# S5 matrices of a hybrid encoder layer kept as 64x64 blocks without zeros, on one Trainium2 core

## The chip, the core and the metric

The kernel runs as one program on one core of a Trainium2 chip. The metric is the device time of one execution in microseconds (us). Before the change the median of three runs is 1902.22 us (1891.05 to 1905.71).

## What is computed

Two layers of an encoder trunk over 528 positions of 1024 channels (16 meta tokens and 512 frames). Each layer projects a normed input into gates and three mixers (gated linear attention, an S5 state space model, sliding window attention), gates and projects each, merges them and adds the result to the residual. The change is in the S5 mixer:

```python
bu_re = einsum('blgi,gni->blgn', ug, bb_re); bu_im = einsum('blgi,gni->blgn', ug, bb_im)
_, _, x_re, x_im = associative_scan(complex_affine_combine, (ab_re, ab_im, bu_re, bu_im), axis=1)
y = einsum('blgn,gin->blgi', x_re, c_re) - einsum('blgn,gin->blgi', x_im, c_im)
y = gelu(y.reshape(B, L, 1024) + d_skip * u)
return y * sigmoid(y @ w_glu)
```

There are 64 groups g of 16 channels i, each with its own complex state of 64 entries n. A group's input matrix is 16 channels to 64 states, its output matrix 64 states to 16 channels. Nothing passes from one group to another.

## The kernel before, in words

**Blocks.** Nearly all of the work is in projections of 1024 by 128 weights, which the program calls blocks. A block's weights come by a DMA that SP issues (`load_block`), ScalarE rounds them (`hi_part`), GpSimd makes the rest (`lo_part`), and TensorE runs 48 matmuls of 264 columns (`project`, L825; L784 and L806 where it follows its input). Three weight buffers are in turn. The list `BLOCKS` sets the order for all engines; each engine runs its own program in that order and waits on semaphores.

**S5 in steps of four.** The scan runs over 132 steps of 4 positions. With the 4 positions folded in, a pair of groups has 2 x 16 channels x 4 = 128 inputs, 2 x 64 = 128 states, and 128 outputs. So each pair (`q` of `QUADS` = 4, eight `j` per layer) has three 128x128 matrices: `mbt` (inputs to states, re and im), `cam` (states to outputs, re and im) and `toep` (inputs of the same step to outputs). Since two groups share one matrix and don't mix, half of each is zero.

**The matrices are built on the core**, for layer 0 in the first blocks (m = 0, during the `gk`, `gv` and `gq` blocks) and for layer 1 at the end of layer 0 (m = 1, after `sg` 2, `ws5` 0, 1, 2, 3, 5 and `wout` 0, 2, 4; `MATS_0`, `MATS_1`). For each j: VectorE (`s5_matrices`) makes products and adds them, per half of the partitions, into `cam` and `mbm`, whose zeros GpSimd has written once, and signals `mats_ready`; TensorE (`step_matrices`, run by `mat_turn` after its block) transposes `mbm` (L881), multiplies `cam` by it (L888, four strips of 32 columns) and turns the next C (L871); ScalarE (`matrices_out`, in its own `mat_turn`) moves both to SBUF and SP spills them to DRAM (`spill_mats`, six DMAs). A buffer is used again when its spill has landed (`spilled`).

**They are used** during the `ag`, `mg2` and `watt` blocks (`S5F`): ScalarE's queue loads the matrices of one j (`load_mats`), TensorE makes the state inputs (`step_inputs`, two `aux` results of 8 matmuls in all, L1164), VectorE scans (`s5_scan`), TensorE makes the outputs (`step_outputs`, 12 matmuls, L1177 and L1179), ScalarE applies the GELU into `Z4` (L1538). In one turn `step_outputs(j)` and `step_inputs(j+1)` follow each other, with two blocks between turns. `AX_` (`aux`) is PSUM in two halves that are taken in turn (`aux_take` waits until the result before last in that half was read).

## Time and profile before

| | |
|---|---|
| median of 3 runs | 1902.22 us |
| the profiled execution | 1898.04 us, of which its span is 1896.2 us |
| TensorE matmuls (PE) | 1762.7 us busy, 93% of the span |
| weight loads (PEld) | 1572.6 us, beside the matmuls |
| VectorE (DVE) | 961.6 us, 51% |
| ScalarE (ACT) | 693.6 us, 37% |
| GpSimd (POOL) | 794.6 us, 42% |
| DMA | 230.38 MB, mean 121 GB/s |

The chain of waits goes through TensorE for 66% of the span, VectorE 10%, DMA 7%, GpSimd 6%. TensorE is the bound in most of the span; the places where it stands idle are the ones to look at, and in the stretches where S5 matrices are built or used most of these are found. Each f32 matmul leaves two records of LDWEIGHTS and two of MATMUL in the trace, so that 12 matmuls are 24 records; a transpose leaves one.

### The profile page before, as it was taken

How to read it: one execution, taken by the hardware profiler on the slowest of the kernel's cores; microseconds unless marked ns; L12 is line 12 of the kernel's file. 1: busy time of each engine (PE TensorE's matmuls, PEld its weight loads, DVE VectorE, ACT ScalarE, POOL GpSimd, SP SyncE). 2: the span in 40 equal slices, each digit the busy share in tenths (PEclk: the TensorE clock that was granted, in tenths of full speed). 3: DMA queues.
4: the chain of work that ended last, by engine and by line, in shares of the span. 5: the costliest groups of instructions: out<-in, count | busy, mean ns of one | idle time of the engine just before them, and what ended most of it. 6: DMA issues, size and time to landing. Idle time of an engine off the chain costs nothing.

```text
span 1896.2 us, 28935 instructions
## 1 busy us (share of the span) xinstructions
PE 1762.7 (93%) x11959; PEld 1572.6 (83%) x11959; DVE 961.6 (51%) x1527; ACT 693.6 (37%) x1236; POOL 794.6 (42%) x492
## 2 busy tenths in 40 slices
PE   6977898999998999999997999989999799999997
PEld 5876798999887999999996987777788688888886
DVE  8997124423428985277653222533243688734223
ACT  3453332444543213233333543344456222224222
POOL 2644565433224324433343686653332332344442
PEclk8898899999999999999998999999999999999999
DMA  9455236222364573436552433542223656433432
GB/s 148 135 167 149 82 88 142 74 79 69 89 152 148 190 200 99 104 90 174 172 156 61 125 90 90 118 123 70 76 79 102 180 191 184 141 100 91 144 104 85
DMA packets 360137, 230.38 MB, mean 121 GB/s; under 512 B 49604, under 2 KB 346744, under 8 KB 357448
## 3 DMA queue, kind: packets, MB, share of 16 engines
q1 hardware_dynamic: 349480, 198.40, 39.8%
q10 hardware_dynamic: 10528, 30.15, 4.7%
q8 instruction: 95, 1.56, 0.4%
q14 instruction: 34, 0.28, 0.1%
HBM read 180.82 MB, written 47.15 MB: 120 GB/s over the span
## 4 chain that ended last, share of the span: by engine, by line
PE 66%; DVE 10%; DMA 7%; POOL 6%; ACT 4%; SPq 3%; issue 3%; ACTq 0%; DVEq 0%; POOLq 0%
PE ring L825 49%; DMA sb_w_raw<-in_w_in 5%; POOL sb_w_lo L667 3%; PE ring L784 3%; DVE sb_s_prod L1572 2%; DVE sb_s_mat_prod L1572 2%; PE aux L1177 2%; PE ring L806 1%; PE aux L1085 1%; SPq L570 1%; PE aux L1164 1%; PE aux L1130 1%; DVE sb_s_rot L2071 1%; PE aux L1106 1%; DVE sb_o_branch L1655 1%
## 5 line engine op out<-in xcount | busy, mean ns | idle before, releaser
L667 POOL TENSOR_TENSOR sb_w_lo<-sb_w_raw,sb_w_hi 128x1024 fp32r<-128x1024 f32 x246 | 608.7, 2476 | 1018.3 <-ACT sb_w_hi L1229 1016.2
L1229 ACT ACTIVATE sb_w_hi<-sb_w_raw 128x1024 fp32r<-128x1024 f32 x246 | 259.9, 1057 | 623.5 <-DMA sb_w_raw<-in_w_in 394.4
L825 PE MATMUL ring<-sb_u_hi,sb_w_hi 128*128 128x264 f32 (+1 forms) x2112 | 362.9, 325 | 31.5 <-DVE sb_tmp_dve L1642 21.4
L825 PEld LDWEIGHTS ring<-sb_u_hi,sb_w_hi 128*128 128x128 f32 x2112 | 308.6, 199 | 70.1 <-DVE sb_tmp_dve L1642 23.8
L825 PE MATMUL ring<-sb_u_lo,sb_w_hi 128*128 128x264 f32 (+1 forms) x2112 | 338.2, 311 | 0.0
L825 PE MATMUL ring<-sb_u_hi,sb_w_lo 128*128 128x264 f32 (+1 forms) x2112 | 334.5, 309 | 0.0
L825 PEld LDWEIGHTS ring<-sb_u_lo,sb_w_hi 128*128 128x128 f32 x2112 | 298.8, 191 | 21.2
L825 PEld LDWEIGHTS ring<-sb_u_hi,sb_w_lo 128*128 128x128 f32 x2112 | 294.2, 188 | 20.9
L1261 ACT ACTIVATE sb_tmp_act<-ring 128x528 f32<-128x528 f32 (+1 forms) x112 | 67.4, 602 | 133.0 <-PE ring L825 130.1
L825 PE MATMUL ring<-sb_y_hi,sb_w_hi 128*128 128x264 f32 (+1 forms) x504 | 88.1, 325 | 3.1 <-ACT sb_w_hi L1229 3.1
L1492 ACT ACTIVATE sb_att_scores<-sb_att_scores,sb_att_neg_max 128x208 f32<-128x208 f32 x128 | 58.4, 458 | 82.1 <-DVE sb_att_neg_max L1860 82.1
L825 PE MATMUL ring<-sb_y_lo,sb_w_hi 128*128 128x264 f32 (+1 forms) x504 | 87.4, 324 | 0.0
L825 PE MATMUL ring<-sb_y_hi,sb_w_lo 128*128 128x264 f32 (+1 forms) x504 | 86.3, 321 | 0.0
L825 PEld LDWEIGHTS ring<-sb_y_hi,sb_w_hi 128*128 128x128 f32 x504 | 73.5, 190 | 10.2 <-issue 3.2
L825 PEld LDWEIGHTS ring<-sb_y_lo,sb_w_hi 128*128 128x128 f32 x504 | 74.7, 192 | 7.3
L825 PEld LDWEIGHTS ring<-sb_y_hi,sb_w_lo 128*128 128x128 f32 x504 | 73.6, 188 | 7.3
L1572 DVE TENSOR_TENSOR sb_y_lo<-sb_o_branch,sb_y_hi 128x528 fp32r<-128x528 f32 (+1 forms) x48 | 50.3, 1065 | 50.7 <-ACT sb_y_hi L1245 50.2
L1677 DVE SCALAR_TENSOR_TENSOR sb_tmp_dve<-sb_tmp_act,ring 128x528 f32<-128x528 f32 (+1 forms) x32 | 22.3, 696 | 98.3 <-PE ring L825 86.1
L1642 DVE SCALAR_TENSOR_TENSOR sb_tmp_dve<-sb_tmp_act,ring 128x528 f32<-128x528 f32 (+1 forms) x32 | 22.2, 694 | 86.0 <-ACT sb_tmp_act L1261 85.5
L1245 ACT ACTIVATE sb_y_hi<-sb_o_branch 128x528 fp32r<-128x528 f32 (+1 forms) x48 | 29.6, 634 | 77.4 <-DVE sb_o_branch L1649 48.7
L1664 DVE SCALAR_TENSOR_TENSOR sb_s_out<-sb_tmp_act,sb_s_out 128x528 f32<-128x528 f32 (+1 forms) x16 | 25.0, 1562 | 63.9 <-ACT sb_tmp_act L1261 63.9
L1677 DVE SCALAR_TENSOR_TENSOR sb_mix<-sb_tmp_act,ring 128x528 f32<-128x528 f32 (+1 forms) x16 | 11.1, 696 | 84.4 <-PE ring L825 76.2
(328 smaller groups left out, 2585.4 us busy)
## 6 DMA issues: line engine op xcount, KB each, us to landing
sb_w_raw<-in_w_in SPq DMA_DIRECT2D x166, 512.0 KB, 4.1
sb_s_loaded<-s_matrices ACTq DMA_DIRECT2D x16, 1808.0 KB, 8.1
s_matrices<-sb_s_phase SPq DMA_DIRECT2D x16, 528.0 KB, 3.2
s_matrices<-sb_s_mbt SPq DMA_DIRECT2D x16, 512.0 KB
s_matrices<-sb_s_ca SPq DMA_DIRECT2D x16, 512.0 KB
sb_w_raw<-in_w_gla_out SPq DMA_DIRECT2D x16, 512.0 KB, 3.8
sb_w_raw<-in_w_attn_out SPq DMA_DIRECT2D x16, 512.0 KB, 3.8
sb_w_raw<-in_s_w_glu SPq DMA_DIRECT2D x16, 512.0 KB, 3.7
```

The lines of the kernel that those rows point to most:

```text
L667: pool.tensor_tensor(WL[:, w], WR[:, w], WH[:, w].bitcast(F32), ALU.subtract).then_inc(lo_ready, 1)
L784: last = pe.matmul(RING[:, 2 * r + hf, 0:c1 - c0], w[:, n % SLOTS, kt, :], moving(b[0], xx[:, kt], c0, c1), start=(term == 0 and kt == 0), ...
L825: last = pe.matmul(RING[:, 2 * r + hf, 0:c1 - c0], w[:, n % SLOTS, kt, :], moving(b[0], xx[:, kt], c0, c1), start=(term == 0 and kt == 0), ...
L1177: pe.matmul(dst, cam[:, ri, q], XX[:, ri, q, :], start=(ri == 0), stop=False)
L1229: act.activation(WH[:, w], WR[:, w], ACT.Copy).then_inc(hi_ready, 1)
L1245: act.activation(YH[:, j, t0:], src[:, t0:], ACT.Copy).then_inc(yhi_ready, 1)
L1261: act.activation(two(TA[:, t % 2], t0), ps, ACT.Tanh, scale=0.5).then_inc(done, 1)
L1492: act.activation(SC[:, u % 2, hd], SC[:, u % 2, hd], ACT.Exp, bias=NMX[:, hd:hd + 1], accum_out=SMM[:, hd:hd + 1])
L1572: return dve.tensor_tensor(o, a, b, op)
L1642: dve.scalar_tensor_tensor(two(td, t0), two(TA[:, t % 2], t0), 1.0, ps, ALU.add, ALU.mult).then_inc(free, 1)
L1664: dve.scalar_tensor_tensor(zj, TA[:, t % 2, t0:].rearrange("p (s c) -> p s c", s=STRIDE), 1.0, zj, ALU.add, ALU.mult).then_inc(glu_used, 1)
L1677: dve.scalar_tensor_tensor(two(td, t0), two(TA[:, t % 2], t0), 1.0, ps, ALU.add, ALU.mult).then_inc(free, 1)
```

## The change

The zeros are left out. The rows of the stationary and moving tiles are ordered by group (64 rows of one group, then 64 of the other) instead of by position, so a pair's matrices become two dense 64x64 blocks each. `mbt`, `cam` and `toep` are half as large (`S5_FLOATS` 3616 before, 2336 now). In pairs with odd `q` the two groups' state halves are exchanged, so that a matmul of an odd pair reads rows of one half and writes the other half. What each engine does instead:

- TensorE: each 128x128 matmul of `step_inputs` and `step_outputs` becomes two of 64x64 with the same 132 columns (16 and 24 in all). `step_outputs` starts with `toep` instead of `cam`, and has three waits on its own semaphore `row_tiles_done`. The eight transposes of `mbm` become 16 matmuls of 64x64 by 64 columns; the eight 32-column matmuls have 64 columns instead of 128 and wait for `first_power`.
- ScalarE: before the old work of a turn, four copies build `mb0`, a small zero-padded copy of `mbm`, and signal `first_power`; the C copies are four instead of two. `load_mats` issues three DMAs instead of one.
- VectorE: two full-height operations in place of four of half height, twice per j; at the start of the program four more copies before `dt_wide`, and six in place of two after it.
- SP, DMAs: `load_b` 8 instead of 2 per layer, `Z4` loads 8 instead of 4, `YD` stores 2 per j instead of 1, `YZ` loads 8 per part instead of 4.
- GpSimd: `cam` and `mbm` need no zeros, `toep` and `mb0` do.

The core of the diff:

```diff
-S5_FLOATS = 2 * QUADS * P + 2 * QUADS * P + QUADS * P + 2 * QUADS * STEPS
+S5_FLOATS = 2 * QUADS * 64 + 2 * QUADS * 64 + 2 * QUADS * STEPS + QUADS * 64
...
+        def load_b(queue, m):
+
+            for ri, src in enumerate((s5_b_re, s5_b_im)):
+                dst = MB[m]["b"][:, ri].rearrange("p (a x) i -> p a x i", x=2)
+                src = src[m].rearrange("(a x g) n i -> x g n a i", x=2, g=2)
+                for g in range(2):
+                    for x in range(2):
+                        rows = slice(S5_STATE * (g ^ x), S5_STATE * (g ^ x) + S5_STATE)
+                        queue.dma_start(dst[rows, :, x], src[x, g]).then_inc(s5_par, 16)
...
                 for ri in range(2):
                     for q in range(QUADS):
-                        last = pe.transpose(AX_[:, 2 * h + ri, P * q:P * q + P],
-                                            MB[m]["mbm"][:, ri, q].rearrange("p a b -> p (a b)"), ID[:])
+                        for g in range(2):
+                            ins, outs = half_rows(g ^ (q % 2)), half_rows(g)
+                            c0 = 128 * ri + 64 * (q // 2)
+                            last = pe.matmul(AX_[outs, 2 * h + q % 2, c0:c0 + 64],
+                                             MB[m]["mbm"][ins, ri, q].rearrange("p a b -> p (a b)"), ID[ins, ins],
+                                             start=True, stop=True)
                 last.then_inc(aux_full[h], 1)
                 h = aux_take(m, ("toep", j))
-                cam, mbm = MB[m]["cam"][:, j % 2], MB[m]["mbm"]
+                cam, mb0 = MB[m]["cam"][:, j % 2], MB[m]["mb0"]
+                pe.wait_ge(first_power, 8 * m + j + 1)
...
+                        for a in range(2):
+                            for x in range(2):
+                                for g in range(2):
+                                    ins, outs = half_rows(g), half_rows(g ^ x)
+                                    last = pe.matmul(AX_[outs, 2 * h + x, STEPS * a:STEPS * a + STEPS],
+                                                     mbt[ins, ri, 2 * a + x, :], Z4[ins, j, 2 * a + x, :],
+                                                     start=True, stop=True)
                         last.then_inc(aux_full[h], 1)
 
                 def step_outputs(j):
 
-                    pe.wait_ge(x_state, 8 * ly + j + 1)
...
+                    for a in range(2):
+                        n = 3 * (8 * ly + j) + 2 * a + 1
+                        if a:
+                            last.then_inc(row_tiles_done, 1)
+                            pe.wait_ge(row_tiles_done, n - 1)
+                        for x in range(2):
+                            for g in range(2):
+                                rows, q = half_rows(g), 2 * a + x
+                                last = pe.matmul(AX_[rows, 2 * h + x, STEPS * a:STEPS * a + STEPS],
+                                                 toep[rows, q], Z4[rows, j, q, :], start=True, stop=False)
+                        last.then_inc(row_tiles_done, 1)
+                        pe.wait_ge(row_tiles_done, n)
+                        pe.wait_ge(x_state, 8 * ly + j + 1)
                         for ri in range(2):
-                            pe.matmul(dst, cam[:, ri, q],
-                                      XX[:, ri, q, :], start=(ri == 0), stop=False)
-                        last = pe.matmul(dst, toep[:, q], Z4[:, j, q, :],
-                                         start=False, stop=True)
+                            for x in range(2):
+                                for g in range(2):
+                                    ins, q = half_rows(g ^ x), 2 * a + x
+                                    last = pe.matmul(AX_[half_rows(g), 2 * h + x, STEPS * a:STEPS * a + STEPS],
+                                                     cam[ins, ri, q], XX[ins, ri, q, :],
+                                                     start=False, stop=(ri == 1))
...
             def matrices_out(m, j):
 
+                act.wait_ge(mats_ready, 8 * m + j + 1)
+                for half in range(2):
+                    rows = slice(64 * half, 64 * half + 64)
+                    for x in range(2):
+                        c0 = S5_GROUP * (half ^ x)
+                        last = act.activation(MB[m]["mb0"][rows, :, x::2, c0:c0 + S5_GROUP],
+                                              MB[m]["mbm"][rows, :, x::2, 0], ACT.Copy)
+                last.then_inc(first_power, 1)
                 if j:
                     spilled(act, m, j - 1)
...
-                act.dma_start(MSB[:, j % 2], MATD[ly, j]).then_inc(mats_in[j % 2], 16)
+                o = S5_FLOATS - QUADS * 64
+                act.dma_start(MSB[:, j % 2, 0:o], MATD[ly, j, :, 0:o]).then_inc(mats_in[j % 2], 16)
+                toep = mat_part(MATD[ly, j], "toep").rearrange("(t g i) x -> g t i x", t=STRIDE, g=2)
+                for g in range(2):
+                    act.dma_start(MSB[64 * g:64 * g + 64, j % 2, o:], toep[g]).then_inc(mats_in[j % 2], 16)
...
-                    for g in range(2):
-                        rows = slice(64 * g, 64 * g + 64)
-                        cols = slice(S5_GROUP * g, S5_GROUP * g + S5_GROUP)
-                        tt(o_re[rows, :, :, cols], t[0][rows], t[1][rows], ALU.subtract)
-                        if negate:
-                            last = dve.scalar_tensor_tensor(
-                                o_im[rows, :, :, cols].rearrange("p q n i -> p (q n) i"),
-                                t[2][rows].rearrange("p q n i -> p (q n) i"), -1.0,
-                                t[3][rows].rearrange("p q n i -> p (q n) i"), ALU.mult, ALU.subtract)
-                        else:
-                            last = tt(o_im[rows, :, :, cols], t[2][rows], t[3][rows], ALU.add)
+                    flat = "p q n i -> p (q n) i"
+                    tt(o_re, t[0], t[1], ALU.subtract)
+                    if negate:
+                        last = dve.scalar_tensor_tensor(o_im.rearrange(flat), t[2].rearrange(flat), -1.0,
+                                                        t[3].rearrange(flat), ALU.mult, ALU.subtract)
+                    else:
+                        last = tt(o_im, t[2], t[3], ALU.add)
                     link(last)
```

TensorE in the second build, from the end of block `ws5` 0 (L784) through its turn to the next block (L825), before (`sb_s_mb` is `mbm`, `sb_s_ca` is `cam`, in brackets the semaphores waited for):

```order
L881 MATMUL aux<-sb_identity,sb_s_mb_134 128x128 [waits aux_free0,mats_ready]
L881 MATMUL aux<-sb_identity,sb_s_mb_134 128x128 x7
L888 MATMUL aux<-sb_s_ca_137,sb_s_mb_134 32x128 [waits aux_free1]
L888 MATMUL aux<-sb_s_ca_137,sb_s_mb_134 32x128 x7
L891 MATMUL aux<-sb_s_skip_diag_144,sb_identity 128x32
L871 MATMUL aux<-sb_identity,sb_s_c_in_143 128x128 [waits c_loaded0]
L871 MATMUL aux<-sb_identity,sb_s_c_in_143 128x128
L825 MATMUL ring<-sb_u_hi,sb_w_hi 128x264 [waits hi_ready,slot_free1]
```

and of the change, at the same place:

```order
L902 MATMUL aux<-sb_identity,sb_s_mb_137 64x64 [waits aux_free0,mats_ready]
L902 MATMUL aux<-sb_identity,sb_s_mb_137 64x64 x15
L911 MATMUL aux<-sb_s_ca_140,sb_s_mb_first_148 32x64 [waits first_power,aux_free1]
L911 MATMUL aux<-sb_s_ca_140,sb_s_mb_first_148 32x64 x7
L914 MATMUL aux<-sb_s_skip_diag_147,sb_identity 128x16
L889 MATMUL aux<-sb_identity,sb_s_c_in_146 128x128 [waits c_loaded0]
L889 MATMUL aux<-sb_identity,sb_s_c_in_146 128x128
L840 MATMUL ring<-sb_u_hi,sb_w_hi 128x264 [waits hi_ready,slot_free1]
```

Between its two groups of matmuls TensorE now waits for ScalarE's `first_power`; the next block stands behind that wait.

ScalarE in the same turn, where its rows now read (`sb_s_mb_first` is `mb0`, `sb_mix_hi` the rounding of the merged sum after block `ws5` 0):

```order
L1271 ACTIVATE sb_w_hi<-sb_w_raw 128x1024 [waits w_loaded0]
L1492 ACTIVATE sb_mix_hi<-sb_mix 128x528 [waits mix_ready]
L1341 ACTIVATE sb_s_mb_first_148<-sb_s_mb_137 64x4x16 [waits mats_ready]
L1341 ACTIVATE sb_s_mb_first_148<-sb_s_mb_137 64x4x16 x3
L1347 ACTIVATE sb_s_mbt_139<-aux 128x2x4x64 [waits aux_full0]
L1351 ACTIVATE sb_s_toep_143<-aux 128x64 [waits aux_full1]
L1365 ACTIVATE sb_s_c_0_144<-aux 64x64 [waits aux_full1,mats_ready]
L1365 ACTIVATE sb_s_c_0_144<-aux 64x64 x3
```

The two rows of L1341 are new; ahead of them stand, as before, a weight block's rounding and a wait for `mix_ready`, which VectorE gives after TensorE has ended block `ws5` 0.

TensorE in the turns of the scan stage (`step_outputs(0)`, then the first half of `step_inputs(1)`), of the change:

```order
L1211 MATMUL aux<-sb_s_steps,sb_s_loaded 64x132 [waits aux_free0]
L1211 MATMUL aux<-sb_s_steps,sb_s_loaded 64x132 x3
L1220 MATMUL aux<-sb_s_state,sb_s_loaded 64x132 [waits x_state,row_tiles_done]
L1220 MATMUL aux<-sb_s_state,sb_s_loaded 64x132 x7
L1211 MATMUL aux<-sb_s_steps,sb_s_loaded 64x132 [waits row_tiles_done]
L1211 MATMUL aux<-sb_s_steps,sb_s_loaded 64x132 x3
L1220 MATMUL aux<-sb_s_state,sb_s_loaded 64x132 [waits x_state,row_tiles_done]
L1220 MATMUL aux<-sb_s_state,sb_s_loaded 64x132 x7
L1193 MATMUL aux<-sb_s_steps,sb_s_loaded 64x132 [waits aux_free1,mats_in1]
L1193 MATMUL aux<-sb_s_steps,sb_s_loaded 64x132 x7
```

Before, these were 12 matmuls of 128x132 behind one wait for `x_state`, then 4; now 24 behind four waits, three of them for TensorE's own matmuls, then 8.

## Rows read from the trace of the kernel before

**Rows 1.** Windows: us; busy us per engine (instructions); TensorE clock, DMA share, GB/s
```profile
84.00:182.00 98.00, 70.06 (x565) 63.75 (x564) 88.96 (x145) 42.62 (x67) 49.69 (x54) 0.85 0.51 143
...
836.00:1010.00 174.00, 167.00 (x1420) 163.00 (x1420) 109.26 (x169) 56.74 (x85) 65.64 (x29) 0.97 0.53 150
```

**Rows 2.** Timeline of TensorE, one turn of the scan stage: start, duration, records
```profile
639.51 0.61 PE L1177 MATMUL aux<-sb_s_state,sb_s_loaded 128*128 128x132 f32 x4
...
642.21 2.03 PE L1164 MATMUL aux<-sb_s_steps,sb_s_loaded 128*128 128x132 f32 x16
643.99 2.18 PE L825 MATMUL ring<-sb_y_hi,sb_w_hi 128*128 128x264 f32 x16
```

**Rows 3.** Lines L888, L1117: ns min/median/max of a record; timeline of narrow matmuls
```profile
L888 PE MATMUL aux<-sb_s_ca,sb_s_mb x256: 272/273/423, 91.2 to 989.9; 128*32 128x128 f32 x128
...
857.67 0.64 PE L888 MATMUL aux<-sb_s_ca,sb_s_mb 128*32 128x128 f32 x16
...
L1117 PE MATMUL aux<-sb_att_pt_a,sb_att_v_a x8: 216/218/264, 384.7 to 384.9; 16*64 16x64 f32 x8
...
384.67 0.45 PE L1117 MATMUL aux<-sb_att_pt_a,sb_att_v_a 16*64 16x64 f32 x8
...
242.24 2.00 PE L992 MATMUL aux<-sb_gla_v_tok,sb_gla_k_tok 64*128 64x256 f32 x16
```

**Rows 4.** Timeline of the scan stage: GELU after an output, second input half waiting
```profile
609.60 0.61 ACT L1538 ACTIVATE sb_s_steps<-aux 128x528 f32<-128x528 f32 x1 [0.26 <-PE aux L1179]
...
626.81 1.17 PE L1164 MATMUL aux<-sb_s_steps,sb_s_loaded 128*128 128x132 f32 x8 [0.18 <-ACT sb_s_steps L1538]
```

**Rows 5.** First build: VectorE's timeline; TensorE's waits in all; chain of waits
```profile
103.92 1.70 DVE L1572 TENSOR_TENSOR sb_s_mat_prod<-sb_s_c,sb_s_powers 128x320 f32<-128x320 f32 x4 [1.95 <-DMA s_matrices<-sb_s_toep]
105.65 0.48 DVE L1572 TENSOR_TENSOR sb_s_ca<-sb_s_mat_prod 64x320 f32<-64x320 f32 x1
...
176.42 1.52 DVE L1572 TENSOR_TENSOR sb_s_mb<-sb_s_mat_prod 64x256 f32<-64x256 f32 x4
...
PE aux L881 <- DVEq L2041: 29.8, 9, 5.8
...
112.48 4.28 DMA s_matrices<-sb_s_toep
```

**Rows 6.** First build: timeline of ScalarE and TensorE after block gv 2
```profile
102.08 1.09 PE L881 MATMUL aux<-sb_identity,sb_s_mb 128*128 128x128 f32 x8 [2.22 <-DVEq L2041]
...
106.81 1.01 ACT L1297 ACTIVATE sb_s_mbt<-aux 128x1024 f32<-128x1024 f32 x1
```

**Rows 7.** Second build: timeline of TensorE
```profile
836.12 3.89 PE L825 MATMUL ring<-sb_u_hi,sb_w_hi 128*128 128x264 f32 x16 [2.93 <-DVE sb_tmp_dve L1642]
...
870.38 1.04 PE L881 MATMUL aux<-sb_identity,sb_s_mb 128*128 128x128 f32 x8
...
922.88 2.73 PE L825 MATMUL ring<-sb_y_hi,sb_w_hi 128*128 128x264 f32 x16 [3.06 <-ACT sb_w_hi L1229]
```

**Rows 8.** Second build: timeline of ScalarE
```profile
859.40 1.01 ACT L1297 ACTIVATE sb_s_mbt<-aux 128x1024 f32<-128x1024 f32 x1
...
873.71 1.01 ACT L1297 ACTIVATE sb_s_mbt<-aux 128x1024 f32<-128x1024 f32 x1
...
874.77 0.55 ACT L1313 ACTIVATE sb_s_c<-aux 64x128 f32<-64x128 f32 x2
...
906.77 1.06 ACT L1229 ACTIVATE sb_w_hi<-sb_w_raw 128x1024 fp32r<-128x1024 f32 x1 [12.67 <-DMA sb_w_raw<-in_w_s_out]
```

**Rows 9.** Start of the scan stage: chain of waits; DMA issues with KB and us to landing
```profile
557.66 13.40 DMA sb_w_raw<-in_w_in
...
sb_s_loaded<-s_matrices ACTq DMA_DIRECT2D x16, 1808.0 KB, 8.1
```

**Rows 10.** Start of the program: timeline of VectorE
```profile
17.53 0.29 DVE L1608 COPY sb_s_params<-aux 128x128 f32<-128x128 f32 x1 [0.93 <-PE aux L944]
...
28.33 0.71 DVE L1615 TENSOR_SCALAR sb_tmp_dve<-aux 128x528 f32<-128x528 f32 x1 [0.25 <-PE aux L847]
```

147 lines of the change are left out of this document (82 added, 65 removed).

## The prediction, made before the changed kernel was run

> **What bounds the kernel now.** I read the page's engine shares first: TensorE is busy for 93% of the span, so a saving on another engine counts only where TensorE waits for it, and TensorE's own records count nearly in full. Then the windows. In the first build (84 to 182 us) TensorE is busy for 70.06 of 98 us at a granted clock of 0.85, VectorE for 88.96: VectorE bounds it. In the second (836 to 1010) TensorE is busy for 167.0 of 174, VectorE for 109.26: TensorE bounds it [rows 1]. In the scan stage the timeline has one turn: outputs from 639.51 to 642.21, inputs to 643.99, then a block without a gap [rows 2]. Last the waits: TensorE waits 29.8 us in nine places for VectorE's `mats_ready` [rows 5]. So three parts of the change can move the end: records on TensorE in the scan stage, VectorE's work in the first build, and in the second whatever puts a wait into a stretch that has nearly none.
>
> The sum is made on the profiled execution (1898.04 us), 4.2 us below the median of the runs.
>
> **Scan stage, records (16 turns).** Outputs take 2.70 us for 24 records and inputs 1.78 for 16 [rows 2]: 0.112 each, together 4.48 a turn. The change has 48 and 32 records, each a 64x64 tile of the same 132 columns. If they didn't overlap at all a turn would take 9 us. The nearest rows say that they do: matmuls of 32 weight columns (four column strips) start (0.64-0.27)/15 = 0.025 us apart with 128 moving columns, those of 64 weight columns (0.45-0.218)/7 = 0.033 [rows 3]. Full overlap of four tiles would be 0.112/4 = 0.028, of two 0.056. I take 0.033 for inputs and `cam` products (32 records each, 1.06 each) and 0.056 for `toep`, which uses only two of the four quadrants (16 records, 0.90): 3.02. To this come three waits of TensorE for itself. Each costs the time from a matmul's start to its end (0.27 by the shortest record of its size [rows 3]) and a restart, which I take as 0.1, in all 0.38: 1.14. I add 0.3 for changes between tile shapes and rounding, which no row shows. 4.46 against 4.48: the turn doesn't get shorter. Bounds: 80 records at 0.028 and no extra make 3.4 (-17 us over 16 turns), all at 0.056 make 5.9 (+23).
>
> The row with 64 weight rows and 256 columns, 16 records in 2.00 us (0.125 each) [rows 3], is at 0.0625 per 128 columns; there two row halves overlap, but they write to two banks of PSUM. In the change both row halves write to one bank in every group of four tiles. No row has that. By the Trainium skill ("TensorEngine Tiling (Array Packing)", Restrictions and Gotchas), different row tiles cannot access one PSUM bank at the same time; by that rule the turn would be the 5.9 and not the 4.46.
>
> **Scan stage, the GELU.** TensorE waits 0.18 us for the GELU of the outputs before it makes the second half of inputs (8 matmuls after the first 8) [rows 4]. The first half lasted 8 x 0.112 = 0.9 and will last 0.5; the outputs end the same. A GELU takes 0.61 and starts 0.26 after TensorE [rows 4]. So the wait grows by what the first half shrinks, 0.4, in 14 to 16 turns: +6. It is lost in full, since the next block stands behind it. Range 0 to +7.
>
> **Loads.** The matrices of one j shrink from 1808 KB, landed in 8.1 us [rows 9], to 2336/3616 of it, 1168 KB. At the start of the scan stage the chain goes for 13.40 us through a weight transfer which lands beside the first matrices [rows 9]. A third of the matrix bytes less: -2 per layer, -4 (0 to -6). Three issues in place of one on ScalarE lie under blocks of TensorE.
>
> **First build (8 matrices).** VectorE writes `ca` and `mb` in half-height operations of 0.48; two full ones replace four, twice: the 0.48 saved twice in each, 1.0 for `ca` and 0.8 for `mb` [rows 5], 1.8 a matrix. At most 14 us. Three things take it back. TensorE's second group of matmuls now needs `first_power`, four copies on ScalarE. After `gv` 2 ScalarE is at 106.81 us with that turn's work, behind the decay's functions, while TensorE was ready at 102.08 [rows 6]; I count a stall of 5 in each of three such turns, partly in place of a wait for the next matrix (5.8 the longest [rows 5]). The next matrix starts not when VectorE is free but when `toep` has been spilled and landed, 4.28 us in the chain, and VectorE waits 1.95 for it [rows 5]: less VectorE time makes that wait longer. And VectorE has ten copies of 0.29 in place of two at the start of the program, with 0.25 us to spare [rows 10]: 8 x 0.29 = 2.3, less that and less some cover by loads, +1.6. Saved are 8 x 1.8 = 14.4; three stalls of 5 come to +15, of which I take off what they replace, waits for the next matrix that shrink by about 4 each, -12; the longer wait for `toep` takes back 8; with the 1.6 the stage ends about 1.5 us earlier (-14.4+15-12+8+1.6 = -1.8). Range -8 to +4. The transposes are 16 records in place of 8, at half the columns: nothing.
>
> **Second build (8 matrices).** Here `first_power` decides. After `sg` 2 and five `ws5` blocks and before the next block TensorE does its turn. After `ws5` 0 the transposes start at 870.38, and ScalarE, which first rounds the merged sum (`mix_ready`), comes to its part at 873.71, 3.3 later [rows 7, 8]. Until now nobody waited for it. Now the four copies come first: about 0.25 each by the C copies of 64x128 (0.55 for two [rows 8]), 1.0 in all, so that TensorE's second group may start 4.3 after the first, of which it fills 1.2: a stall of 3.1. After `sg` 2 (ScalarE's part at 859.40 [rows 8], second group of TensorE at 857.67 [rows 3]) it is 1.7+1.0 = 2.7 less a start that moves with the copies, 2.4. After `ws5` 2, ScalarE stands before a weight block that lands late and is rounded at 906.77 (idle 12.67 [rows 8]); the turn's transposes begin near 900, so the stall is 906.77+1.06+1.0-901 = 8. For the other turns I take, by the nearest of these, 3.1 after `ws5` 1, 2.4 after one more, and 1 after each of two `wout`, where ScalarE is free and its copies run beside the transposes: 2.4+3.1+3.1+8+2.4+1+1 = 21, one turn at nothing. Taken off: waits of TensorE for VectorE and ScalarE in this stage which the new stall covers. They are 2.93 and 3.06 with slowed blocks behind them (3.89 and 2.73 for the 16 records that take 2.18 elsewhere [rows 2, 7]), and 1.9 of `mats_ready`: -8. Idle stretches of 2.9 and more are followed by blocks at the low clock, which I charge the new ones of 3.1 and 8 with 2. The sum is 21-8+2 = 15; I take +14, since a delay of one turn leaves ScalarE more time before the next. Range +2 (ScalarE is waited for only for the 1.0 of its copies, and the 8 taken off) to +25 (nothing taken off).
>
> **Costed at nothing:** `load_b`, `Z4`, `YD` and `YZ` issues, hidden by blocks (SP stands in no wait of TensorE in the rows); GpSimd's zeros, in its idle time; 32 narrow records in a build turn, the same columns in all.
>
> **Sum.** 0 + 6 - 4 - 1.5 + 14 = +14: 1898 + 14 = **1912 us**.
>
> **Rivals.**
> 1. *Forecast*: stalls for `first_power` outweigh VectorE's saving, and the scan stage gives nothing. 1912, own range 1898 to 1924. Chance 0.50.
> 2. *The quadrants overlap in full and ScalarE is in time.* For it: 0.025 is in a row already. Scan turn 2.2+1.1 = 3.3 instead of 4.46, -18, GELU +8, loads -5, first build -5, second +5: 1883 (1872 to 1893). Against: ScalarE's late starts are in the rows. Chance 0.18. This one ends faster.
> 3. *Two row halves do not write to one bank together.* Every record of the scan stage costs 0.056: 80 x 0.023 less the `toep` already so priced, 64 x 0.023 = 1.5 a turn, +23 on the forecast, less 3 of the GELU's 6, as the first half of the inputs covers it again: 1932. Its place is `step_inputs` and the `cam` products. It decides from 0.045 a record on, where +12 is reached. For it the skill's rule above; against it nothing, as all rows have separate banks. Chance 0.20. It ends slower.
> 4. *The wait feeds back.* In the second build ScalarE's rounding of the next weights stands behind its copies, TensorE behind both, and six of the turns lose 3 and as much as a slowed block (1.7, from 3.89 against 2.18 [rows 2, 7]), with one more of 8, less the 8 taken off: +28 in place of +14: 1926. It decides from a ScalarE that comes 2.9 late in four turns or more. Chance 0.12.
> 5. *It doesn't do what it says*: weights of 64 rows load no faster, so a record costs 0.112 and nothing overlaps. 9 us a turn: +72, 1980. The rows of L888 and L992 speak against it; left out of the range.
>
> **How the numbers follow.** Range 1884 to 1936: half of case 2 lies below or at its end, cases 3 and 4 mostly inside, case 5 outside. A difference of 1% (19 us) is what a measurement can tell from no change, so faster is below 1883 and slower above 1921. Faster: half of case 2, 0.10. Slower: case 3 with 0.18, case 4 with 0.08, an eighth of case 1, 0.06, in all 0.32. The rest, 0.58, is within.
>
> **What would show it.** In the trace after: (a) TensorE waiting for ScalarE's copy L1341 at L911 in the second build, about 20 us in all over eight places, and the window from `sg` 2 to `wout` 4 some 14 us longer; (b) records of L1193 and L1220 0.033 apart and the turn about 4.5 us; 0.056 is case 3, 0.028 case 2; (c) a wait for the GELU of about 0.6 before the second half of L1193; (d) VectorE's busy time lower by 1.8 per matrix (29 us over both builds), while the first build ends within a few us of 182. I am wrong if ScalarE's copies run before TensorE's transposes end in most turns, or if the first build shrinks by 8 us or more, which would mean that the spill of `toep` wasn't what held VectorE.

## The result, and the profile after

The changed kernel takes 1921.5 us (median of 4 runs, 1920.58 to 1929.08) where the kernel before, run beside it, takes 1900.86. The ratio is 1.0107, with a 95% interval of 1.0081 to 1.0132: slower by 1.1%. One run of the experiment e3 below (2004.83 us) was slower at a lower clock and is left out of its row. The forecast was 1912 us, +14 on the profiled execution; the measured time is inside the range, 9 us above its middle. The profiled execution has a span of 1918.8 us against 1896.2, +22.6.

The page's engine shares show less work, not more, on TensorE and VectorE:

```profile
span 1918.8 us, 31149 instructions
...
PE 1748.8 (91%) x12985; PEld 1539.8 (80%) x12985; DVE 930.4 (48%) x1471; ACT 701.7 (37%) x1332; POOL 787.4 (41%) x490
```

TensorE is busy for 14 us less than before and the span is 22.6 longer, so TensorE stands idle for some 36 us more. The waits of TensorE (engine, line, whom for: us in total, times, longest) say where:

```profile
PE aux L911 <- ACT sb_s_mb_first L1341: 32.3, 12, 6.3
PE ring L840 <- DVE sb_tmp_dve L1707: 19.9, 8, 6.1
PE aux L1193 <- DMA sb_s_steps<-s_in_rows: 17.3, 2, 9.3
...
PE aux L902 <- DVEq L2102: 12.3, 4, 5.6
```

Two entries are new: `first_power`, 32.3 us, which the forecast had, and the loads of `Z4`, 17.3 us, which it had costed at nothing (before, TensorE waited 0.4 for them in layer 0, and 1.4 at the same place in layer 1). The wait for `mats_ready` fell from 29.8 [rows 5] to 12.3.

Following the same event through both timelines gives the account. Each number is how much later (+) the event comes than before:

| event | before, us | later by | this stretch |
|---|---|---|---|
| first block | 35.64 | +2.7 | +2.7 |
| last `mbm` transposes of the first build | 178.32 | -3.3 | -6.0 |
| TensorE ready for the first `step_inputs` | 569.2 | -9.0 | -5.7 |
| first `step_inputs` (569.64 before) | 569.64 | -1.4 | +7.6 |
| last `step_outputs` of layer 0 | 724.98 | -0.6 | +0.8 |
| first `mbm` transposes of the second build | 856.71 | -1.0 | -0.4 |
| last of them | 988.59 | +13.2 | +14.1 |
| block before layer 1's `step_inputs` | 1482.63 | +14.7 | +1.5 |
| its first `step_inputs` | 1486.02 | +22.7 | +8.0 |
| end | 1896.2 | +22.6 | -0.1 |

The second build cost 14.1, and two waits for `Z4` cost 15.5. All else together is -7, and not all of that is the change's: in e3 below, whose program is that of before up to the `Z4` loads, TensorE is ready at 565.98 and so 3.2 us earlier than before. The windows that answer to [rows 1], with the columns given there:

```profile
84.00:182.00 98.00, 70.33 (x810) 66.93 (x809) 77.81 (x117) 50.24 (x115) 55.22 (x58) 0.84 0.41 108
...
836.00:1010.00 174.00, 156.69 (x1526) 153.79 (x1527) 88.78 (x136) 55.84 (x122) 58.33 (x24) 0.93 0.41 115
```

In the first build VectorE has 11 us less to do (88.96 before), TensorE gets no further for it. In the second, TensorE's busy share is down from 167.0 to 156.7, and its clock from 0.97 to 0.93. The timeline there, the turn after block `ws5` 0, answers to [rows 7, 8]; first TensorE:

```profile
873.19 0.69 PE L902 MATMUL aux<-sb_identity,sb_s_mb 64*64 64x64 f32 x32
876.54 0.43 PE L911 MATMUL aux<-sb_s_ca,sb_s_mb_first 128*32 128x64 f32 x16 [2.65 <-ACT sb_s_mb_first L1341]
...
877.31 3.72 PE L840 MATMUL ring<-sb_u_hi,sb_w_hi 128*128 128x264 f32 x16
```

and ScalarE:

```profile
875.05 0.64 ACT L1492 ACTIVATE sb_mix_hi<-sb_mix 128x528 fp32r<-128x528 f32 x1 [3.04 <-DVE sb_mix L1627]
875.60 0.79 ACT L1341 ACTIVATE sb_s_mb_first<-sb_s_mb 64x64 f32<-64x64 f32 x4
```

ScalarE waits for the merged sum until 875.05, rounds it, then makes `mb0`. TensorE stood since 873.9. The 16 records behind the wait take 3.72 us and not 2.18 [rows 2]: they ran mostly at the low level of the clock (1.2 GHz), as the granted clock of 0.54 in that stretch shows (third last number, here and in the other windows):

```profile
877.30:881.00 3.70, 3.70 (x20) 3.70 (x19) 3.63 (x8) 1.82 (x6) 1.39 (x1) 0.54 0.44 121
```

So a wait of 2.65 costs 4.2 here. The turn after `ws5` 2, where ScalarE stands before a late weight block, is the longest:

```profile
915.06 0.65 PE L911 MATMUL aux<-sb_s_ca,sb_s_mb_first 128*32 128x64 f32 x16 [6.30 <-ACT sb_s_mb_first L1341]
```

The scan stage's turn of [rows 2], in the changed kernel:

```profile
640.79 0.67 PE L1211 MATMUL aux<-sb_s_steps,sb_s_loaded 64*64 64x132 f32 x8
641.53 0.68 PE L1220 MATMUL aux<-sb_s_state,sb_s_loaded 64*64 64x132 f32 x16
642.30 0.67 PE L1211 MATMUL aux<-sb_s_steps,sb_s_loaded 64*64 64x132 f32 x8
643.03 0.68 PE L1220 MATMUL aux<-sb_s_state,sb_s_loaded 64*64 64x132 f32 x16
643.53 0.63 PE L1193 MATMUL aux<-sb_s_steps,sb_s_loaded 64*64 64x132 f32 x16
644.44 0.68 PE L1193 MATMUL aux<-sb_s_steps,sb_s_loaded 64*64 64x132 f32 x16 [0.28 <-ACT sb_s_steps L1593]
645.05 2.22 PE L840 MATMUL ring<-sb_y_hi,sb_w_hi 128*128 128x264 f32 x16
```

A record takes 0.273 us from start to end (median of L1220). So 16 records in 0.68 or 0.63 start (0.68-0.27)/15 = 0.027 apart, or 0.024: four tiles at once. The eight `toep` records are (0.67-0.27)/7 = 0.057 apart: two. From the last start of one group to the first of the next are 641.53-(640.79+7x0.057) = 0.34 us, which is the price of one of TensorE's own waits. From the last start of the first half of the inputs (643.53+0.63-0.27 = 643.89) to the first start of the second half are 0.55 us: the wait for the GELU, 0.28 behind the end of the last matmul, costs about 0.5 in starts. The whole turn is 645.05-640.79 = 4.26 us against 4.48.

The first `step_inputs`, after TensorE stood for the loads, and SP's queue (start, length, issues) as it issues them:

```profile
568.25 2.04 PE L1193 MATMUL aux<-sb_s_steps,sb_s_loaded 64*64 64x132 f32 x32 [7.99 <-DMA sb_s_steps<-s_in_rows]
```

```profile
540.88 9.22 SPq L621 DMA_DIRECT2D sb_s_steps<-s_in_rows  x8
```

SP's eight issues take 9.2 us where four took 4.7, but not 1.15 us each (ns min/median/max, before and after):

```profile
L610 SPq DMA_DIRECT2D sb_s_steps<-s_in_rows x8: 318/646/2604, 549.9 to 1468.0; - x8
...
L621 SPq DMA_DIRECT2D sb_s_steps<-s_in_rows x16: 319/487/2877, 540.9 to 1488.7; - x16
```

The first five take 0.32 to 0.49 us, and only the last three 1.9 to 2.4, while the earlier loads are under way. What is long is the loads: in layer 0 from the first issue to the last landing 27.3 us (540.88 to 568.19), where before they took 19.7 (549.89 to 569.60), and in layer 1 28.0 against 13.7. A window of 8 us while the loads run, of before (issues from 549.89) and of after:

```profile
551.00:559.00 8.00, 8.00 (x67) 7.62 (x64) 0.59 (x1) 1.94 (x3) 2.39 (x1) 1.00 1.18 190
```

```profile
551.00:559.00 8.00, 8.00 (x68) 8.00 (x67) 0.00 (x0) 0.00 (x0) 0.00 (x0) 1.00 1.26 115
```

The last column is GB/s: 190 with loads of 32 partitions, 115 with loads of 16, and the DMA engines are taken up in both (1.18 and 1.26).

### The profile page after: what moved, and what is told of

It is laid out like the page before. It is cut to its first block, busy times and chain, and to the rows that moved or that the text cites. A ratio compares the mean times of both kernels' runs of the same rounds, so it can differ in the third digit from the quotient of the medians.

```text
span 1918.8 us, 31149 instructions
## 1 busy us (share of the span) xinstructions
PE 1748.8 (91%) x12985; PEld 1539.8 (80%) x12985; DVE 930.4 (48%) x1471; ACT 701.7 (37%) x1332; POOL 787.4 (41%) x490
## 4 chain that ended last, share of the span: by engine, by line
PE 65%; DVE 12%; POOL 6%; DMA 6%; ACT 5%; issue 3%; SPq 3%; ACTq 0%; DVEq 0%; POOLq 0%
PE ring L840 50%; DMA sb_w_raw<-in_w_in 4%; POOL sb_w_lo L682 3%; PE ring L799 3%; DVE sb_s_prod L1627 3%; PE ring L821 2%; PE aux L1111 1%; DVE sb_s_rot L2132 1%; SPq L579 1%; DVE sb_s_rot L1627 1%; PE aux L1220 1%; SPq L621 1%; DVE sb_s_state L1627 1%; PE aux L1132 1%; PE aux L1156 1%
## 5 line engine op out<-in xcount | busy, mean ns | idle before, releaser
L840 PE MATMUL ring<-sb_u_hi,sb_w_hi 128*128 128x264 f32 (+1 forms) x2112 | 372.1, 331 | 29.6 <-DVE sb_tmp_dve L1707 19.9
L840 PEld LDWEIGHTS ring<-sb_u_hi,sb_w_hi 128*128 128x128 f32 x2112 | 317.1, 204 | 69.3 <-DVE sb_tmp_dve L1707 22.4
L1729 DVE SCALAR_TENSOR_TENSOR sb_s_out<-sb_tmp_act,sb_s_out 128x528 f32<-128x528 f32 (+1 forms) x16 | 21.7, 1355 | 67.7 <-ACT sb_tmp_act L1303 67.7
L1627 DVE TENSOR_TENSOR sb_s_mat_prod<-sb_s_bbar,sb_s_powers 128x256 f32<-128x256 f32 x64 | 48.5, 818 | 11.0 <-PE aux L889 10.5
```

Of the source, the lines that this page charges most:

```text
L840: last = pe.matmul(RING[:, 2 * r + hf, 0:c1 - c0], w[:, n % SLOTS, kt, :], moving(b[0], xx[:, kt], c0, c1), start=(term == 0 and kt == 0), ...
L1627: return dve.tensor_tensor(o, a, b, op)
L1729: dve.scalar_tensor_tensor(zj, TA[:, t % 2, t0:].rearrange("p (s c) -> p s c", s=STRIDE), 1.0, zj, ALU.add, ALU.mult).then_inc(glu_used, 1)
```

## The experiments

Times and ratios of all, each against runs of the kernel before on the same chip:

| kernel | median us | before beside it | ratio (95%) |
|---|---|---|---|
| changed | 1921.50 | 1900.86 | 1.0107 (1.0081 to 1.0132) |
| e1 `mb0` by VectorE | 1899.35 | 1904.33 | 0.9979 (0.9961 to 0.9996) |
| e2 `Z4` on two queues | 1916.37 | 1904.33 | 1.0058 (1.0026 to 1.0091) |
| e3 before, `Z4` in eight | 1916.26 | 1904.33 | 1.0074 (1.0040 to 1.0109) |
| e4 `Z4` in rows | 1898.32 | 1904.33 | 0.9963 (0.9942 to 0.9983) |
| e5 e1 and e4 | 1875.81 | 1904.32 | 0.9855 (0.9821 to 0.9889) |
| e6 before, `Z4` in rows | 1905.73 | 1904.32 | 1.0010 (0.9988 to 1.0032) |
| e7 e5, half heights | 1893.14 | 1904.32 | 0.9935 (0.9912 to 0.9957) |
| e8 rows, 16 partitions | 1930.20 | 1904.32 | 1.0144 (1.0110 to 1.0178) |
| e9 e1, copies kept | 1902.92 | 1902.63 | 0.9990 (0.9973 to 1.0008) |
| e10 e5, early copies | 1872.81 | 1902.63 | 0.9840 (0.9813 to 0.9866) |
| e11 e5 again | 1876.56 | 1902.63 | 0.9855 (0.9831 to 0.9879) |

A hundredth of the ratio is 19 us.

**e1: no wait for `first_power`.**

```diff
                 h = aux_take(m, ("toep", j))
-                pe.wait_ge(first_power, 8 * m + j + 1)
...
                 products(BB[:, :, qs], 4, MBM[:, 0], MBM[:, 1], False)
+                for half in range(2):
+                    rows = slice(64 * half, 64 * half + 64)
+                    for x in range(2):
+                        c0 = S5_GROUP * (half ^ x)
+                        dve.tensor_copy(MB[m]["mb0"][rows, :, x::2, c0:c0 + S5_GROUP], MBM[rows, :, x::2, 0])
```

and ScalarE's four copies with their wait are gone.

> The changed kernel, but VectorE writes mb0 (four 64x64-element copies behind its other work of a matrix, before mats_ready), and TensorE's wait for first_power is gone. Theory: the 16.9 us that TensorE waits for ScalarE's copies in the second build (five waits, 2.6 to 6.3 us) are the whole loss of that stage, so it gets about 14 us shorter again; in the first build the 15 us of such waits partly turn back into waits for VectorE, which has 8 x 4 short copies more (3 to 5 us): 0 to -4. In all about 1905 us, ratio to the kernel before 1.001 to 1.004. Rival: TensorE would have stood there anyway (for mats_ready, for weights that come late): then the waits move to other lines and the time stays within 5 us of the changed kernel, ratio above 1.008.

1.0107 became 0.9979, about -24 us: more than I expected, and far from the rival. The turn of above is now

```profile
865.16 0.69 PE L902 MATMUL aux<-sb_identity,sb_s_mb 64*64 64x64 f32 x32
865.79 0.43 PE L910 MATMUL aux<-sb_s_ca,sb_s_mb_first 128*32 128x64 f32 x16
...
866.56 2.20 PE L840 MATMUL ring<-sb_u_hi,sb_w_hi 128*128 128x264 f32 x16
```

without a gap and at full clock. From the first to the last transposes the second build takes 124.3 us (851.99 to 976.31), against 146.0 in the changed kernel and 131.9 before. So `first_power` cost 21.7 there, and what the stage saves otherwise, hidden behind it, is 7.6. About half of the 7.6 is in the turns themselves: from the transposes to the next block are 1.40 us (865.16 to 866.56) where before they were 1.96 (870.38 to 872.34), 0.56 in each of seven turns. Waits for `mats_ready` of 1.9 us in all are gone too. In the first build the same stretch went from 86.8 to 78.9 us, 89.0 before; I had expected at most 4 us there.

**e9: ScalarE's copies kept, the wait taken away.** As e1, but ScalarE still makes four copies per matrix, of a constant into a buffer that nobody reads.

```diff
-                        last = act.activation(MB[m]["mb0"][rows, :, x::2, c0:c0 + S5_GROUP],
-                                              MB[m]["mbm"][rows, :, x::2, 0], ACT.Copy)
+                        last = act.activation(MB[m]["spare"][rows, :, x::2, c0:c0 + S5_GROUP],
+                                              ID[rows, 0:64].rearrange("p (r a i) -> p r a i", r=2, a=2), ACT.Copy)
```

> As the kernel in which VectorE writes mb0, but ScalarE still does its four copies per matrix (of a constant, into a buffer nobody reads), and TensorE doesn't wait for them. Theory: it is the wait that costs, with the low clock behind it, not the 0.8 us of ScalarE's time per matrix: like e1, ratio to the kernel before 0.996 to 1.000. Rival: the copies make ScalarE's weight roundings late, and that is what stopped TensorE: then at least half of the 22 us comes back, ratio above 1.003.

0.9990, with an interval that overlaps that of e1: at most a few of the 24 us are ScalarE's own time. It is the wait that costs.

**e3: the kernel before with the `Z4` loads alone in eight.**

```diff
-                            sp.dma_start(Z4[32 * p:32 * p + 32].rearrange("i j q c -> i (j q) c"),
-                                         ZD[ly, :, :, STRIDE - 1 - p, :].rearrange("j (q i) c -> i (j q) c", q=QUADS)
-                                         ).then_inc(steps_loaded, 16)
+                            for g in range(2):
+                                r0 = 32 * p + 16 * g
+                                sp.dma_start(Z4[r0:r0 + 16].rearrange("i j q c -> i (j q) c"),
+                                             ZD[ly, :, :, STRIDE - 1 - p, :]
+                                             .rearrange("j (q g i) c -> g i (j q) c", q=QUADS, g=2)[g]
+                                             ).then_inc(steps_loaded, 16)
```

> The kernel before, with one edit: each of its four Z4 loads of 32 partitions is issued as two of 16 partitions. Theory: this edit alone costs what the changed kernel loses there, 8 us per layer where the wait was 0.4 and 0: +8 to +16 us, ratio 1.004 to 1.009. Rival: the wait comes from the matrix loads in pieces of 256 bytes, or from TensorE's having been early (by 9 us in layer 0) only: then the time is that of the kernel before within 3 us.

+0.7%, 14 us, from an edit that moves the same bytes to the same places. TensorE's waits for these loads:

```profile
PE aux L1167 <- DMA sb_s_steps<-s_in_rows: 18.8, 2, 9.6
```

**e2: the eight loads on two queues.** The four of the second half are issued by ScalarE, beside SP's.

```diff
-                        for g in range(2):
+                        for g in range(1):
                             for p in range(STRIDE):
...
+                        for p in range(STRIDE):
+                            r0 = 64 + 16 * p
+                            act.dma_start(Z4[r0:r0 + 16].rearrange("i j q c -> i (j q) c"),
+                                          ZD[ly, :, :, STRIDE - 1 - p, :]
+                                          .rearrange("j (q g i) c -> g i (j q) c", q=QUADS, g=2)[1]
+                                          ).then_inc(steps_loaded, 16)
```

> The changed kernel, but of the eight Z4 loads the four of the second row half are issued from ScalarE's queue, at the same time as SP issues the other four. Theory: the waits of 8.0 and 9.3 us for Z4 at the start of the scan stage come from transfers of 16 partitions, one after the other on one queue, at 100 to 125 GB/s in place of 180; two queues have 32 partitions under way, and the waits fall to below 1 us, less what later work takes: -12 to -17 us, ratio 0.999 to 1.004. Rival 1: only SP's issue time (9.2 us in place of 4.7) matters: then the same, but the rate during the loads stays at 100 to 125 GB/s and the wait keeps 3 to 4 us each. Rival 2: the DMA engines bound it, whatever the queue: under 4 us in all, ratio above 1.008.

TensorE waits as long as in the changed kernel:

```profile
PE aux L1193 <- issue: 16.6, 2, 8.9
```

But it no longer waits for `Z4`. SP's four issues take 1.91 us, and the last `Z4` load lands at 564.40 (ScalarE's, issued at 546.56), 5.5 us before TensorE's first matmul at 569.87; in layer 1 it is 1502.65 and 1507.06. From the first issue to the last landing the loads take 21.6 and 23.2 us in place of 27.3 and 28.0. What is left for TensorE to wait for is `mats_in`: the first matrices, which ScalarE now issues behind its four `Z4` loads, from 550.69 on, and whose last packet ends at 569.01. (In the changed kernel their last packet ends at 567.29, 0.9 us before the last `Z4` load lands, so that little more than that was to be had here.) So the run doesn't settle how far two queues help. While both move `Z4` the rate is

```profile
550.00:554.00 4.00, 4.00 (x35) 4.00 (x34) 1.41 (x2) 0.61 (x1) 1.09 (x1) 1.00 1.24 141
```

141 GB/s: more than the 108 to 115 of the one queue, and far from 190. None of the three expectations came as stated: the waits are as long as the second rival has them, but for another reason than the `Z4` loads, and the ratio of 1.0058 lies below its 1.008. The ratio is 0.5% lower than the changed kernel's, with intervals that overlap, and I can't say whether anything of that is real. For two transfers to separate halves the Trainium skill ("DMA: Bandwidth & Descriptors", Rules for kernel authors) says that they share the same engines, so "Use one 128-partition transfer"; e4 does so, with 10.9 us from the first issue to the last landing against 21.6 here.

**e4: the same data in four loads of 128 partitions.** The inputs are spilled in the order of `Z4`'s rows, so that a load can take all rows.

```diff
-                            sp.dma_start(ZD[ly, j], Z[:, j]).then_inc(z_spilled, 16)
+                            for t in range(STRIDE):
+                                sp.dma_start(ZD[ly, QUADS * j:QUADS * j + QUADS, :, STRIDE - 1 - t]
+                                             .rearrange("q g i c -> (q g) i c"), Z[:, j, t]).then_inc(z_spilled, 16)
...
+                        for j in range(0, KT, 2):
+                            sp.dma_start(Z4[:, j:j + 2].rearrange("r j q c -> r (j q) c"),
+                                         ZD[ly, QUADS * j:QUADS * j + 2 * QUADS]
+                                         .rearrange("b g t i c -> (g t i) b c")
+                                         ).then_inc(steps_loaded, 16)
```

> The changed kernel, but the spilled S5 inputs lie in DRAM in the order of Z4's rows, so that Z4 comes in four loads of 128 partitions (two j each) in place of eight of 16; the stores before it are 32 of 66 KB in place of 8 of 264 KB. Theory: the loads run at 180 GB/s or more and cost SP under 5 us, so both waits (8.0 and 9.3) go: -13 to -18 us, ratio 0.998 to 1.003. Rival: the four stores of the last j land later and the load is bound by its 528-byte pieces whatever its partitions: under 5 us, ratio above 1.008.

-27 us on the changed kernel by the ratios. TensorE's wait for these loads is gone. The loads were issued from 546.23 on and landed by 557.08, and the window in which they run reads

```profile
548.00:554.00 6.00, 6.00 (x52) 6.00 (x51) 1.28 (x2) 0.61 (x1) 1.73 (x1) 1.00 1.18 310
```

310 GB/s. The gain is more than the 15.5 us of waits. The weights of the next blocks stand behind these loads on SP's queue and in the DMA engines. It fits this that from the first `step_inputs` to the first `step_outputs` are 34.6 and 33.4 us in the two layers, where the changed kernel has 38.7 and 37.2; but it wasn't tried apart.

**e8: partitions or place in DRAM?** The new order in DRAM, but eight loads of 16 partitions; the diff is against e4.

```diff
-                        for j in range(0, KT, 2):
-                            sp.dma_start(Z4[:, j:j + 2].rearrange("r j q c -> r (j q) c"),
+                        for g in range(2):
+                            for t in range(STRIDE):
+                                r0 = 64 * g + 16 * t
+                                sp.dma_start(Z4[r0:r0 + 16].rearrange("i j q c -> i (j q) c"),
+                                             ZD[ly, :, g, t].rearrange("b i c -> i b c")
```

> The changed kernel with the new spill order in DRAM, but still eight loads of 16 partitions each (each row piece 528 bytes as in all versions; 16 rows are now neighbours in DRAM). Theory: the number of partitions of a load sets its rate, not where its pieces lie in DRAM: both waits stay (7 to 10 us each), total within 5 us of the changed kernel, ratio 1.007 to 1.012. Rival: neighbouring pieces in DRAM were what made the four loads fast: the waits fall below 2 us, ratio 0.995 to 1.001.

```profile
547.00:553.00 6.00, 6.00 (x52) 6.00 (x51) 1.41 (x2) 0.61 (x1) 1.36 (x1) 1.00 1.25 111
```

The place in DRAM isn't what made e4's loads fast: in loads of 16 partitions the rate is back at 111 GB/s, the waits are 23.6 us, and the ratio is 1.0144. That is a little above the 1.012 I had as the upper end, as the waits of 11.5 and 12.0 us are above my 10. (The loads are also half as large as e4's; size and partitions weren't varied apart.)

**e5 and e11: both mends.** Their diffs are those of e1 and e4.

> The changed kernel with both edits that helped: VectorE writes mb0 (no wait for first_power), and Z4 is loaded in four loads of 128 partitions from inputs spilled in row order. Theory: the two losses lie in different stages, so their mends add up: -22 and -23 us on the changed kernel, about 1877 us where the kernel before takes 1901, ratio 0.985 to 0.989. Rival: both made TensorE earlier at the same later wait (the weights of the scan stage, VectorE's scan), and only one of them counts in full: ratio above 0.992.

> The kernel with both mends once more, beside e10 on the same chip: 0.983 to 0.989 of the kernel before, as the first time.

0.9855 twice. The two add up (-0.0128 and -0.0144 give 0.9835, which lies inside both intervals), and this version beats the kernel before by 1.5%, 27 us.

**e6: the new spill order in the kernel before.** So that the gain isn't put down to the wrong edit.

```diff
+                            for t in range(STRIDE):
+                                sp.dma_start(ZD[ly, QUADS * j:QUADS * j + QUADS, STRIDE - 1 - t], Z[:, j, t]
+                                             ).then_inc(z_spilled, 16)
...
+                                         .rearrange("b t i c -> (t i) b c")
```

> The kernel before with the new spill order alone (32 stores of 66 KB, then four loads of 128 partitions per layer), everything else as it was. Theory: the four loads of 32 partitions cost the kernel before little (waits of 0.4 and 0 us for them), but they hold up the weights behind them by some 4 us in each layer: -4 to -10 us, ratio 0.995 to 0.998. So what is left between this kernel and the one with both mends (about 15 us) is what the dense tiles are worth. Rival: the loads of 32 partitions were as fast as any, then nothing: 0.999 to 1.002.

1.0010: nothing, and my expectation of -4 to -10 us was wrong. In layer 0 the loads of 32 partitions had landed just as TensorE came (0.42 us of wait), so there was hardly a wait to take away. Here SP's stores before the loads take 7.0 us, the loads are issued 1.7 later than before, and TensorE waits 4.6 us for them in all; that the stores are the reason wasn't tried apart. So the 1.5% of e5 isn't the new order's, to within the 0.3% that this interval leaves: it is the dense matrices', once they are freed of the two waits.

**e7: VectorE's half heights again, in e5.**

```diff
-                    tt(o_re, t[0], t[1], ALU.subtract)
+                    for g in range(2):
+                        rows = slice(64 * g, 64 * g + 64)
+                        tt(o_re[rows], t[0][rows], t[1][rows], ALU.subtract)
```

and the same for `o_im`.

> The kernel with both mends, but VectorE does the last two operations of each product per half of the partitions again, as before the change (8 operations in place of 4 per matrix). Theory: it costs 1.8 us per matrix on VectorE; in the first build VectorE is what TensorE waits for (21 us of such waits with ScalarE's out of the way), so 8 to 14 us come back there, in the second build under 3: +9 to +15 us on the kernel with both mends, ratio to before 0.991 to 0.995. Rival (my count of the prediction, where the landing of the spilled toep set the pace): +1 to +4 us.

0.9935: +15 us, the upper end of what I expected and far from what the prediction had counted. VectorE on one product, in e5:

```profile
104.35 0.49 DVE L1618 TENSOR_TENSOR sb_s_ca<-sb_s_mat_prod 128x320 f32<-128x320 f32 x1
104.76 0.48 DVE L2080 SCALAR_TENSOR_TENSOR sb_s_ca<-sb_s_mat_prod 128x320 f32<-128x320 f32 x1
...
106.74 0.76 DVE L1618 TENSOR_TENSOR sb_s_mb<-sb_s_mat_prod 128x256 f32<-128x256 f32 x2
107.54 0.60 DVE L2096 COPY sb_s_mb_first<-sb_s_mb 64x64 f32<-64x64 f32 x4
```

and in e7 the two `ca` operations are four of 0.48, the two `mb` 1.53. An operation of half the partitions costs the same, 0.48 or 0.49, so that 0.9+0.8 a matrix are saved. TensorE's waits for `mats_ready` are 22.0 us in e5 and 33.8 in e7, and the first build (first to last transposes) 79.6 and 89.3. So about half of the gain of e5 (0.0080 of 0.0145, each known to 0.003) lies in this one edit.

**e10: the early copies.** In e5, VectorE's five copies of S5 rows at the start stand ahead of its parameter copy; in the changed kernel one of them takes 2.35 us in place of 0.18, beside GpSimd's first two `lo_part` (14.64 to 19.29):

```profile
16.99 2.35 DVE L1662 COPY sb_s_rows_swapped<-sb_s_rows 128x64 f32<-128x64 f32 x1
```

```diff
             dve.drain().then_inc(h_ready, 9)
+            dve.wait_ge(s5_rows, 16 * (2 * DEPTH + 1))
+            dve.tensor_copy(LDB[:], LDR[:].unsqueeze(2).broadcast_to([DEPTH * PAIRS, 2, S5_STATE]))
...
+            last.then_inc(dt_wide, 1)
             h = aux_result(dve, -1, ("prm", 0))
```

> The kernel with both mends, and VectorE's five copies of the S5 parameter rows at the start stand ahead of its parameter and bias copies, where they don't meet GpSimd's first two weight remainders (one of the copies took 2.35 us there in place of 0.18). Theory: the first block starts 2 to 4 us earlier than with both mends (it started 2.5 later than in the kernel before), and half of it is left at the end: -1 to -3 us on e11. Rival: VectorE's wait for the first matrix or the weights takes it all: 0.

The first block starts 2.1 us sooner than in e11 (36.45 and 38.57). 0.9840 against 0.9855 points the same way, but the intervals overlap: not settled. 1872.81 us is the lowest median of all.

## Why the prediction came out as it did

The direction and the mechanism of `first_power` were right. That the total lies inside the range is partly luck: 15.5 us that no term had, from the `Z4` loads, stand against a scan stage and a first build that did better than forecast. By its terms:

- **Second build, +14 forecast, +14.1 measured.** Five waits in place of seven: 2.62, 2.65, 2.61, 6.30 and 2.68, 16.9 in all where I had 21; none in the `wout` turns, where I had 1 each. The slowed blocks behind them (3.50, 3.72, 3.47, 3.04 and 3.19 us in place of 2.20) took 5.9 where I had 2. The gross price was 21.7 (e1 against the changed kernel), what the stage saved otherwise 7.6, where I had taken 8. That these two agree is luck: my 8 was waits alone, and I had counted the narrow records of a turn as nothing saved, while they save 0.56 a turn. (I also had 16 records for the dense transposes; the trace has 32, in 0.69 us where 8 took 1.04 [rows 7].) The price of the wait is shown by e1, and by e9 that it isn't ScalarE's time.
- **First build, -1.5 forecast, -3.3 at its last transposes.** Three longer `first_power` waits came, of 5.74, 4.55 and 1.56 us where I had 5 each; the one that I had read from rows, after `gv` 2, is the 1.56, with a wait of 5.19 for `mats_ready` ahead of it. With four of about 0.9 they filled nearly what VectorE gave: 27.9 us of waits for `mats_ready` before, 12.3 for it and 15.4 for `first_power` now. But I had put 8 us of VectorE's saving under the landing of `toep`. That was wrong, though VectorE's busy time fell as forecast (961.6 to 930.4, 31 us where I had 29): VectorE's products waited 3.8 us for it before and 1.3 in the changed kernel; e1 has the build 10.1 us shorter than before, and e7 gives 15 us back when only VectorE's operations are halved again. Another 5.7 us came between 178 and 569. Over 3 of them can be chance, as e3 shows; a block that had run slowly at 305.91 (3.48 us) took 2.20 now. I had not looked past the end of the build.
- **Start, +1.6 forecast, +2.7 measured.** The copies themselves were cheap; one took 2.35 beside GpSimd's `lo_part`, and e10 starts 2.1 sooner with the copies moved away from there.
- **Scan stage, records, 0 forecast (4.46 a turn where it was 4.48), about -0.7 a turn measured.** The turn of 4.26 us holds about 0.5 of the GELU's wait, so that the records and TensorE's own waits are 3.8. Inputs and `cam` are at 0.027, not 0.033; `toep` at 0.057, as taken; own waits 0.34 to 0.36, not 0.38; and of the 0.3 for changes of tile shape hardly anything came. So the dense tiles overlap in full, and yet the outputs are no shorter (2.74 us, 640.79 to 643.53, against 2.70): 48 records cost 16x0.057+32x0.027 = 1.8 in place of 2.70, and three waits of 0.35 take it back. The gain is in the inputs, about 1.0 in place of 1.78.
- **Scan stage, the GELU, +6 forecast, about +6 measured.** In 12 turns the wait is 0.28, and about 0.5 counted in starts. It takes back most of what the inputs gave, as the prediction said. TensorE waits for VectorE's state for 8.9 us against 5.9 (`toep` goes first, so these waits now stand in front of `cam`). From the first outputs to the last the stage is 0.8 us shorter in layer 0 and 1.7 in layer 1. (The table's +0.8 for layer 0 starts at the first inputs: 1.6 came in between inputs and outputs.)
- **Rival 3 is ruled out** by the trace alone. In each group of four tiles both row halves write one bank, on different partitions, and records start 0.027 apart. Against it stood the rule of the Trainium skill ("TensorEngine Tiling (Array Packing)", Restrictions and Gotchas) that different row tiles cannot access one bank at the same time; the measurement decides, for tiles that write different partitions. For tiles that write the same partitions of a bank nothing was tried: the kernel's waits keep them apart.
- **`Z4` loads, costed at nothing, +15.5 measured in waits.** This is the step that failed. I named SP's queue as hidden by blocks, since SP stood in no wait of TensorE. But the timelines of the kernel before show the loads and who waits for them, SP's queue and TensorE:

```profile
549.89 4.67 SPq L610 DMA_DIRECT2D sb_s_steps<-s_in_rows  x4
```

```profile
569.64 2.07 PE L1164 MATMUL aux<-sb_s_steps,sb_s_loaded 128*128 128x132 f32 x16 [0.42 <-DMA sb_s_steps<-s_in_rows]
```

A wait of 0.42: in layer 0 the loads landed just on time, so every us more on them was in the open. I had taken a short wait for cover. (In layer 1 they had landed 5.0 us before TensorE came, which then waited 1.4 for the first matrices.) What makes them long is the rate, 190 GB/s with 32 partitions and 115 with 16. SP's own time for the issues is at most a part of it: with SP done after 1.91 us in e2, the loads still took over 21.
- **Matrix loads, -4 forecast.** Not seen apart: the `Z4` waits cover their place, and in e2 the matrices' own landing is what TensorE waits for. It wasn't tried alone.
- **Rivals 2 and 4.** Rival 2 had the records right (0.028) and ScalarE wrong, which wasn't in time. Rival 4 had it right that a slowed block stands behind each wait, but in five turns and not seven, and 14.1 us is half of its 28. That the time lies between the forecast's 1912 and rival 4's 1926 is the work of `Z4`, which is in neither.

## What to carry to other kernels

Ask of each new wait when the engine that signals it comes to that place in its own order, and not how long its operation takes: four copies of 0.8 us in all cost 22 us in one stage. Look for transfers that land just as they are needed, since a wait of 0.4 us means that there is nothing to spare; splitting such a transfer by partitions is no small matter. And when a change loses, mend its waits one by one before it is dropped: here the same idea was 1.5% faster.
